# One decoder layer on one NeuronCore: the sample stage with its keys taken into the head pairs and its values in four quarters

## The reference

```python
qa, ka, va, qb, kb, vb, qi, ki, wi, logf, ga, gb = project(h, w_in, ...)
# prompt: mixer A (sparse, ALiBi) and mixer B (forgetting), 8 heads of 64 each
# sample, for each of the 8 sequences and each mixer:
kb_all = concat([paged_rows(cache_k_b), kb]); vb_all = concat([paged_rows(cache_v_b), vb])
F = cumsum(concat([paged_rows(cache_logf_b), logf]))
ob = softmax(q . k * HEAD_DIM**-0.5 + F[past] - F) @ v      # forget_attend
oa = the same with -slope*distance on the selected rows      # sparse_attend
merged = sigmoid(ga) * (oa @ w_o_a) + sigmoid(gb) * (ob @ w_o_b)
x = x + gate1 * (merged @ w_out)
x = x + gate2 * (relu(h2 @ w_up) ** 2 @ w_down)
```

## Time and profile before

| | |
|---|---|
| median of 3 runs | 1105.62 us (1105.55 to 1106.54) |
| the profiled execution | 1111.2 us, of which 1109.3 are its span |
| PE, DVE, ACT, POOL busy | 90%, 48%, 39%, 15% of the span |
| granted PE clock, mean | 0.946 |
| moved by DMA | 124.55 MB, mean 112 GB/s |

### The profile page before, as it was taken

The page is one execution under the profiler, slowest core; times in us unless marked ns, Lnnn a source line. Parts: engine busy times, 40 slices in busy tenths (PEclk is TensorE's granted clock), DMA queues, the critical chain, the costliest instruction groups (busy, mean ns, idle before and its releaser), DMA issues.

```text
span 1109.3 us, 20087 instructions
## 1 busy us (share of the span) xinstructions
PE 999.1 (90%) x7616; PEld 907.8 (82%) x7616; DVE 531.2 (48%) x1206; ACT 427.8 (39%) x867; POOL 165.7 (15%) x129
## 2 busy tenths in 40 slices
PE   8798878898999999549899999599989999998998
PEld 7596756777888789546499999589989999998998
DVE  3545677566354533652058744654423234442332
ACT  3345454455576652112154544334421114441111
POOL 3001222222352233220003222000000000000000
PEclk9899889899999999769979999799999999999999
DMA  9431512212222226784436665222323332332312
GB/s 349 143 83 31 163 53 74 67 49 58 77 56 70 78 55 201 228 257 137 155 108 197 201 180 177 65 74 83 91 76 95 95 90 82 93 95 77 94 58 77
DMA packets 184107, 124.55 MB, mean 112 GB/s; under 512 B 14419, under 2 KB 168083, under 8 KB 184036
## 3 DMA queue, kind: packets, MB, share of 16 engines
q1 hardware_dynamic: 183906, 123.50, 37.3%
q10 hardware_dynamic: 130, 0.10, 0.0%
HBM read 116.99 MB, written 6.59 MB: 111 GB/s over the span
## 4 chain that ended last, share of the span: by engine, by line
PE 72%; DVE 11%; DMA 4%; SPq 3%; issue 3%; ACT 3%; POOL 2%; ACTq 0%; DVEq 0%; POOLq 0%
PE bank L880 19%; PE bank L881 18%; PE bank L882 18%; DMA qbc<-q_d 3%; PE bank L964 2%; PE bank L1140 2%; PE bank L987 2%; PE bank L973 1%; POOL prod L787 1%; PE bank L799 1%; SPq L572 1%; DVE sel L1807 1%; PE bank L1005 1%; PE bank L821 1%; DVE w_lo L1757 1%
## 5 line engine op out<-in xcount | busy, mean ns | idle before, releaser
L880 PE MATMUL bank<-h_hi,w_hi 128*128 128x260 f32 x1360 | 405.6, 298 | 31.6 <-DVE h_lo L1700 17.7
L881 PE MATMUL bank<-h_lo,w_hi 128*128 128x260 f32 x1360 | 393.7, 289 | 0.0
L882 PE MATMUL bank<-h_hi,w_lo 128*128 128x260 f32 x1360 | 393.0, 289 | 0.0
L880 PEld LDWEIGHTS bank<-h_hi,w_hi 128*128 128x128 f32 x1360 | 266.0, 196 | 55.9 <-issue 47.3
L881 PEld LDWEIGHTS bank<-h_lo,w_hi 128*128 128x128 f32 x1360 | 266.5, 196 | 0.2
L882 PEld LDWEIGHTS bank<-h_hi,w_lo 128*128 128x128 f32 x1360 | 266.1, 196 | 0.0
L880 PE MATMUL bank<-u_hi,w_hi 128*128 128x260 f32 x512 | 146.7, 287 | 7.7 <-DVE u_lo L2151 7.7
L756 POOL TENSOR_TENSOR w_lo<-raw,w_hi 128x1024 fp32r<-128x1024 f32 x42 | 100.0, 2380 | 345.0 <-ACT w_hi L1335 178.5
L881 PE MATMUL bank<-u_lo,w_hi 128*128 128x260 f32 x512 | 146.3, 286 | 0.0
L882 PE MATMUL bank<-u_hi,w_lo 128*128 128x260 f32 x512 | 146.2, 286 | 0.0
L2136 DVE TENSOR_TENSOR w_lo<-raw,w_hi 128x1024 fp32r<-128x1024 f32 x62 | 76.0, 1226 | 145.7 <-ACT w_hi L1575 145.7
(11 more groups left out here) (319 smaller groups left out, 1308.5 us busy)
## 6 DMA issues: line engine op xcount, KB each, us to landing
raw<-in_w_in SPq DMA_DIRECT2D x44, 512.0 KB, 3.7
raw<-in_w_ada SPq DMA_DIRECT2D x32, 512.0 KB, 3.9
raw<-in_w_up SPq DMA_DIRECT2D x32, 512.0 KB, 3.9
raw<-in_w_down SPq DMA_DIRECT2D x32, 512.0 KB, 3.8
ada<-in_w_ada SPq DMA_DIRECT2D x4, 2048.0 KB, 12.8
kv<-in_cache_k_b SPq DMA_DIRECT2D x16, 256.0 KB, 3.0
qbc<-q_d SPq DMA_DIRECT2D x16, 256.0 KB, 4.3
kv<-in_cache_k_a SPq DMA_DIRECT2D x16, 256.0 KB, 3.2
```

The source lines that it names most:

```text
L880: mm(out, hi[:, k, :], x_h, start=first and k == ks[0], stop=False)
L881: mm(out, hi[:, k, :], x_l, start=False, stop=False)
L882: end = mm(out, lo[:, k, :], x_h, start=False, stop=last and k == ks[-1])
```

## The change

Six things are changed together.

1. Queries of the sample group are stored as soon as they are normalized (`query_store`), and keys and queries 0 to 13 are loaded at listed slots of pairs 6 to 9 (`PAGES_AT`, `QUERY_AT`). Three key buffers are in rotation, so the pages of n wait for sum n-3; the query of n waits for product n-2.
2. Products are made in place, 12 on POOL and 4 on DVE, at listed slots (`POOL_KEYS_AT`, `DVE_KEYS_AT`); sums 0 to 10 stand in DVE's queue in the slots of `SUMS_AT`. In pair 8 and after it the weight remainders are DVE's instead of POOL's.
3. The two mixers share one softmax on 128 rows; what doesn't need the keys is made ahead (`spread_rows`, `rows_ready`). `turn_rows` stands ahead of tile +8.
4. Values are loaded into six buffers and multiplied in four batches ahead of tiles +10, +11, +13 and +14, each batch four units in four groups of 32 columns.
5. `sample_outputs` stands ahead of tile +15, with 12 calls for 16.
6. ACT takes the sigmoids in the loop of the gate tiles.

```diff
-KEYS_AT = [0, 2, 3, 3, 2, 3, 3]
-VALUES_AT = {15: 2 * NS}
+POOL_KEYS = [0, 1, 2, 3, 4, 5, 6, 7, 8, 10, 12, 14]
+DVE_KEYS = [9, 11, 13, 15]
+POOL_KEYS_AT = [(6, 5), (6, 7), (7, 0), (7, 2), (7, 3), (7, 5), (7, 6), (8, 0), (8, 7), (9, 1)]
+DVE_KEYS_AT = [(9, 0), (9, 2)]
+SUMS_AT = [(6, 7), (7, 0), (7, 1), (7, 3), (7, 4), (7, 6), (7, 7), (8, 1), (9, 1), (9, 3), (9, 4)]
+PAGES_AT = [(6, 2), (6, 2), (6, 2), (7, 0), (7, 1), (7, 2), (7, 4), (7, 5), (7, 7), (8, 0), (8, 2), (9, 2), (9, 3), (9, 4)]
+QUERY_AT = [(6, 3), (6, 3), (6, 6), (7, 0), (7, 1), (7, 3), (7, 4), (7, 6), (8, 5), (8, 5), (9, 0), (9, 1), (9, 2), (9, 3)]
+BATCHES_AT = [10, 11, 13, 14]
...
+            def load_keys(n):
+                if n == 0:
+                    sp.wait_ge(lg_ready, 8 * 4)
+                if n >= 3:
+                    sp.wait_ge(prod_used, n - 2)
+                load_pages(kv[n % 3], "cache_k_", n // NS, n % NS, kv_landed[n % 3])
+
+            def load_query(n):
...
+                if n >= 2:
+                    wait_product(sp, n - 2)
+                sp.dma_start(qbc[n % 2][:, :], q_d[n // NS, n % NS].partition_broadcast(P)).then_inc(qbc_landed[n % 2], 16)
...
+            sample_stores(1)
+            load_keys(14)
+            load_query(14)
+            load(T_GATE + 11)
+            load_keys(15)
+            load_query(15)
+            for v in range(3):
+                load_values(v)
+            load(T_GATE + 12)
...
+            def product(n):
+                wait_keys(pool, n)
+                pool.tensor_tensor(kv[n % 3][:, :, :], kv[n % 3][:, :, :], qbc[n % 2][:, :].unsqueeze(1).to_broadcast([P, NPAGE, SEQ]), ALU.mult)\
+                    .then_inc(prod_pool, 1)
...
-                    last = mm(bank[2 + m][0:64, :], ptz[:, NPAGE * m + pg, 64 * b:64 * b + 64], vbuf[v % 4][:, pg, :],
-                              start=b == 0 and pg == 0, stop=b == NS - 1 and pg == NPAGE - 1)
+                    for j in range(4):
+                        v = 4 * t + j
+                        if pg == 0:
+                            pe.wait_ge(val_landed[v % 6], 16 * NPAGE * (v // 6 + 1))
+                        last = mm(bank[3][32 * j:32 * j + 32, :], ptz[:, 4 * pg + j, 32 * t:32 * t + 32], vbuf[v % 6][:, pg, :],
+                                  start=t == 0 and pg == 0, stop=t == 3 and pg == NPAGE - 1)
...
+                if p >= N_PAIRS:
+                    for i in split_at(p, s):
...
+                        rest_w(i)
...
+                if i == T_GATE + 5:
+                    key_sum(11)
+                    product(13)
+                    key_sum(12)
+                if i == T_GATE + 6:
+                    key_sum(13)
+                    product(15)
+                    rows_ready()
+                if i == T_GATE + 7:
+                    key_sum(14)
+                    key_sum(15)
+                if i == T_GATE + 8:
+                    rows_logits()
+                    rows_probs()
...
+                if i == T_GATE + 14:
+                    own_features()
                 rest_w(i + 2)
```

More of the change, by code:

```diff
@@ L116, in dma_count, with batch_unit @@
     return 2 if T_WO <= i < T_WO + NCH * GROUP and not is_ada(i) else 1
-def unit_tile(n, slots):
-    for tile, count in slots:
-        if n < count:
-            return tile
-        n -= count
+def batch_unit(v):
+    t, j = v // 4, v % 4
+    return j // 2, 4 * (j % 2) + t
 def landed_value(i):
@@ new lines, in _ @@
+            load(T_GATE + 13)
+            load_values(4)
+            load_values(5)
+            load(T_GATE + 14)
+            load(T_GATE + 15)
+            for v in range(6, 10):
+                load_values(v)
+            load(T_WO)
+            for v in range(10, 14):
+                load_values(v)
+            load(T_WO + 1)
+            load(T_WO + 2)
+            for v in range(14, 2 * NS):
+                load_values(v)
+            for i in range(T_WO + 3, T_MLP):
+                load(i)
@@ new lines, in spread_rows, with turn_rows @@
+                for m in range(2):
+                    mm(bank[7][64 * m:64 * m + 64, 0:H], spread[:, :], s8[:, 9 + m, :], start=True, stop=True)
+                mm(bank[7][0:64, 16:16 + H], spread[:, :], sm_tok_s[:, ROW_FL:ROW_FL + H], start=True, stop=True).then_inc(rows_turned, 1)
+            def turn_rows():
+                pe.wait_ge(side_read, len(SIDE))
+                pe.wait_ge(prod_used, 2 * NS)
+                for pg in range(NPAGE):
+                    last = tr(bank[2][:, pg * P:(pg + 1) * P], lgs[:, pg].rearrange("p m r -> p (m r)"), ident[:, :])
+                last.then_inc(rows_turned, 1)
@@ L1375, in store_gate @@
                     act.wait_ge(k_stored, 16 * N_PAIRS)
+                if j >= 9:
+                    act.wait_ge(prod_used, 2 * NS)
+                if j >= 10:
+                    A(gate[:, j, half * HALF:(half + 1) * HALF], bank[half + 4 * par(i)][:, 0:HALF], ACT.Sigmoid).then_inc(act_evac, 1)
+                    return
                 A(gate[:, j, half * HALF:(half + 1) * HALF], bank[half + 4 * par(i)][:, 0:HALF], ACT.Copy).then_inc(act_evac, 1)
@@ L2034, in rows_probs @@
[L2034 to L2041 removed]
+                if (p, s) in DVE_KEYS_AT:
+                    product(DVE_KEYS[DVE_KEYS_AT.index((p, s))])
```

365 lines of the change are left out of this document (173 added, 192 removed).

## The result

| | before | after |
|---|---|---|
| median of the runs | 1105.76 us (4 runs) | 1073.24 us (4 runs, 1071.99 to 1077.89) |
| ratio | | 0.9712, 95% interval 0.9682 to 0.9743 |
| profiled execution, span | 1111.2, 1109.3 | 1074.34, 1072.5 |
| pairs: from the value product twelfth from the last to the last one | 84.9 | 94.1 |
| stage: last value product to first output projection | 145.6 | 103.0 |

The account below looks back on a forecast made before the run. TensorE, busy 90% of the span, bounds the kernel, but in the sample stage it waits behind the key chain. Stage -56 and pairs +7 give -49 us from 1105.6, said as 1056; own range 1048 to 1066, 8 in 10 1042 to 1075.

Parts of the forecast that it names:

- the second rival: Head pairs: mutual exclusion stops DVE at ten products and each reaches PE, 24 us instead of 7, 1073; chance 0.16.
- signs of being wrong: Profile after: value matmuls above 0.2; two or three large waits at tiles +7 to +9; head pairs slower by over 5 each.
- Values, 7.6 us: Stage: 64 value matmuls in four column quarters overlap at 0.119 each, 7.6 us instead of 27.7, gain 20.1.
- The rival with quarters that don't overlap: Stage's value matmuls: the four quarters give no overlap, +20 us, 1076; chance 0.05.
- Outputs, 3.1 us: Stage: sample outputs as 24 matmuls at full clock ahead of the last gate tile, 0.13 each, 3.1 us, gain 5.3.
- The 8 us wait before turning the rows: Stage, after tile +7: PE, ready at 435.7, waits 8 us for the last key sum at 443.5.
- So nearly no wait here; I write 0.5.: Stage, before tile +7: DVE's remainder done at 429.6, PE ready at 429.5, so a wait of 0.5 us.
- Query 15, 4.3 to 5.6 us: Stage, key 15: its query broadcast lands after 4.3 us in the median, 5.58 in the chain, about 436.
- The end, 0.6 us: Stage's end: the 3.3 us wait for masked features goes, and a wait of 0.6 us is kept.
- The stage's sum: Stage: tiles 62.9, values 7.6, outputs 3.1, short products 2.4, slow tile 2.8, waits 10.6; 89.4 against 145.6 us.
- The pairs, 7 us: Head pairs: 1.6 + 1.5 + 3.2 + 1.5 + 1 = 8.8 us lost, less about 2 of small waits, 7 us.
- The rivals without cost or slower: No cost in pairs, last keys in time: 1050 or 1039, chance 0.12; products stop PE, 64 us: 1114, chance 0.03.

Follow-up runs that it names:

- kernel 3: Changed kernel with all 64 value matmuls writing the first 32 columns, one quarter instead of four; 1091.84 us, one run, stage 117.4.
- traces 1: Changed kernel with POOL's ten key products in the head pairs multiplying 64 of the 512 columns; 1069.09 us, one run, pairs 90.5.
- Kernel 2: Changed kernel with DVE's key sums 0 to 7 adding 8 of each head's 64 products; 1067.56 us, one run, pairs 89.6.
- 9: Changed kernel with POOL's products 0 and 4 held until their pair's keys are written and sums 3 to 6 later; 1071.12 us, one run.
- Kernel 4: Changed kernel with the weight remainder of tile +7 ahead of product 13 on DVE; 1068.73 us, ratio 0.9648 to the kernel before.
- kernel 10: Changed kernel with own buffers for keys 13 and 15, outputs' low half early, and key pages and values ahead of weights in SP's queue; 1052.40 us (0.9514).
- kernel 8: Changed kernel with the loads of values 0 to 2 behind the weights of tiles +12 and +13; 1069.53 us, one run.
- kernel 7: Changed kernel with own buffers for keys 13 and 15, remainder of +7 ahead of product 13, and outputs' low half ahead of a weight remainder; 1059.15 us (0.9567).
- kernel 11: kernel 10 with held products and later sums in the pairs, and sums 14 and 15 ahead of the rows' preparation; 1043.54 us (0.9404).
- kernels 5: Changed kernel with own page buffers for keys 13 and 15 and an own query buffer for key 15; 1061.67 us, one run.

## Why the prediction was right, and where 12 us went

The time lies in the range of 1042 to 1075, and the forecast's own case came true in kind: the gain is in the stage, and the pairs pay. But the gain was sized 49 and is 36.9 between profiled executions, and 1073.24 lies outside the 1048 to 1066 that the forecast gave its own case. It falls on the 1073 of the second rival, whose mechanism did not come true; that is a coincidence. Of its signs of being wrong one came: two large PE waits, at tiles +7 and +8, with DVE behind pages at the first and behind a query at the second. Another came for one pair of three: pair 7 was over 5 us slower. So the kind was right, and that the wide range held is in part luck.

By stretches, the stage gave 42.6 instead of 56, the pairs took 9.2 instead of 7, and 3.4 more came from outside both (1.9 ahead of the pairs' stretch, 1.4 behind the stage), which the forecast had at nothing; executions differ there by more than that.

- **Values, 7.6 us.** Right: 16 matmuls in 1.92 us, and kernel 3 shows that it is the four quarters that do it (0.44 in one, 0.12 in four). The rival with quarters that don't overlap is refuted.
- **Outputs, 3.1 us.** Right (3.3 to the next tile). What was overlooked is the tile behind them, partly at half clock and 1.6 us longer by it, without a wait.
- **The 8 us wait before turning the rows.** Right in size (7.9) and releaser, with DVE idle before product 15 for a query. But its walk was wrong: it came to 8 from a last sum at 443.5 and PE ready at 435.7; measured are 457 and 449.3. Both ends moved by the same 13.5: 7.2 by the pairs, and 6.4 mostly by the wait before +7 and the slow tile behind it on PE, and on the key chain by the late remainder (4.9) and the late query. So the wait itself hid the error, and that it came out at 8 is luck.
- **"So nearly no wait here; I write 0.5."** This is the step that failed. Before tile +7 PE waited 4.7. The walk had pages 13 issued at 421.8 and landed 4.0 later, which is 429.0 and 433.0 with the 7.2 us by which the pairs end later. They were issued at 429.65, near where the walk had them, but landed at 436.23: 6.6 us, with pages 12, a query and weights issued in the 3 us ahead of them, and stores, pages 14 and a query in the 3.5 us behind (5.6 to 6.7 in traces 1, 2, 3 and 9; which of the neighbours costs it was not tried). That is 3.2 of the 4.9 us that the remainder came late. Most of the rest is the remainder itself, 3.17 instead of 1.26 beside a POOL product: the mechanism that the text used for the pairs was not applied to the stage. Kernel 4 shows that the remainder's place behind the pages makes the wait, kernel 10 that DVE need not wait for pages there at all.
- **Query 15, 4.3 to 5.6 us.** 6.65. It needed both the values behind it and the weights just ahead: 4.3 without the first (kernel 8), 4.7 with the weights earlier (kernel 4).
- **The batches' waits, 1.5 us.** Batches 1 and 3 took 4.4 more than batches 0 and 2, for values behind weights in SP's queue (kernel 10).
- **The end, 0.6 us.** 2.9. The low half of the outputs stood on DVE behind a weight remainder that waits for tile +15 (kernel 7). The change had put the outputs ahead of that tile, and the text took the whole chain behind them along; the order of DVE's queue was not walked through.
- **The stage's sum.** Forecast 89.4, measured 103.0, 13.6 more: waits before +7, at turn_rows and at the end 6.4, batches 2.7, three slow tiles instead of one 2.7, and 2.0 from eleven full-clock tiles at 5.9 from start to start where 48 by 0.119 had given 5.7; outputs and short products make up the last 0.2 down.
- **The pairs, 7 us.** 9.2. In pair 6 product 0 holds the gain multiplication and PE waits 1.83, as forecast; but the clock stays at 1.00 behind this wait, so the 1.5 for half clock did not come, and the pair lost 1.4. Pair 7 was put mainly on products (3.2 + 1.5) and lost 6.5. The 2.2 for product 5 beside the gain multiplication did not happen (0.69 at 369.53). Instead PE waited 2.10 for probabilities and 1.36 for o_lo, around which lie the 3.7 us between the ninth- and eighth-last value product, and then 1.23 for the keys, with the clock at half around them (0.50 from 369 to 372), 2.8 more. Kernel 2 shows that the sums in DVE's queue, of which the forecast priced one, take part in that as much as the products or more. Pair 8 was put at 1 and lost 1.1.
- **The rule of the Trainium skill**, page "SBUF — State Buffer", section "Who interferes with whom". In kind the traces agree again, in 2.74, 2.51 and 3.17 us for DVE multiplications and subtractions of 1.23 beside POOL's. The rival that it spoke for, 24 us for ten products, is refuted: without the products the pairs are 3.6 shorter, so most of what they stop does not reach PE. The same section says that on this chip tensor_scalar can in some modes take the shared ports too, and that a reduction never does. With 1.05 to 1.31 us for the mean squares' 8 numbers (0.17 alone) and an unchanged 0.69 for the reduction ahead of them, the traces agree.
- **The rivals without cost or slower** are out: the pairs did pay, and the ten products cost 0.4 us of PE's time each, far from the 5.6 at which the change would lose.

## What to carry to other kernels

Walk every in-order queue on the way of a late operand, the issuing queue first: here the largest step of the later kernels, 8.8 us of the stage, came from loads that had stood behind other loads whose wait had nothing to do with them, and twice one cheap instruction, put ahead of a wait instead of behind it, brought 2.5 and 6.5 us. A wait that is forecast right in size proves little, since both of its ends can be late by as much. Where work moves beside other work, price its place in the queue as well as its hold on another engine; here either, cut alone, gave about 4 us, partly by the same wait.

## What the runs showed of the hardware that was not expected

- A DVE instruction of 8 numbers in each of 128 partitions, with one input, took 1.05 to 1.31 us when it started beside a POOL instruction, ending 0.03 us behind that one's end, and 0.17 alone; the one of a single number beside POOL's (kernel 11, 358.08) stayed at 0.15.
- 24 short matmuls (3.4 us at full clock, no wait before or in them) were followed by TensorE at about half clock, for 3 to 7 us, in eleven of the twelve traces with all 24 ahead of a tile: 0.57 over 4 us in the changed kernel. In kernels 5, 7 and 11 (0.55 over 6 us) the clock fell within the last of them already. In two groups with half a tile between, the clock stayed at 1.00. In kernel 3 it stayed there too with all 24 together, so this is not a rule.
- A 256 KB query broadcast took 6.65 us with weights and two pages issued in the 1.5 us ahead of it and six value pages in the 4.5 us after it, 4.3 without the six (kernel 8), and 4.7 with the six but the weights 4.9 us ahead (kernel 4).
